# Gate sums of a two-block decoder kernel: both fp16 parts in one TensorE product of 176 columns, joined by ScalarE and VectorE

## What is computed

```python
        q = (xb @ w_query).astype(jnp.float32).reshape(t, PEER_HEADS, 2, PEER_HALF)
        scores = jnp.einsum("thpc,hpkc->thpk", q, sk)
        s1, i1 = lax.top_k(scores[:, :, 0], PEER_TOPK)
        s2, i2 = lax.top_k(scores[:, :, 1], PEER_TOPK)
        ...
        idx = jnp.take_along_axis(cand_idx, top_pos, axis=-1)
        gate = jax.nn.softmax(top_s, axis=-1)
        u = expert_down[idx]
        v = expert_up[idx]
        act = jax.nn.gelu(jnp.einsum("td,thkd->thk", xb, u).astype(jnp.float32), approximate=False)
        return jnp.einsum("thk,thkd->td", (gate * act).astype(v.dtype), v)
```

## Time and profile before

| | |
|---|---|
| Runs | 1342.95, 1343.41, 1344.96 us; median 1343.41 us |
| Profiled execution | 1341.96 us, span of its instructions 1340.2 us |
| Busy in the span | TensorE 98%, its weight loads 90%, VectorE 70%, ScalarE 54%, GpSimd 37% |
| Mean granted TensorE clock | 0.994 of full speed |

### The profile page before, as it was taken

The page is one execution under the profiler, slowest core; times in us unless marked ns, Lnnn a source line. Parts: engine busy times, 40 slices in busy tenths (PEclk is TensorE's granted clock), DMA queues, the critical chain, the costliest instruction groups (busy, mean ns, idle before and its releaser), DMA issues. The chain is left out here.

```text
span 1340.2 us, 25360 instructions
## 1 busy us (share of the span) xinstructions
PE 1314.9 (98%) x8845; PEld 1200.1 (90%) x8845; DVE 943.3 (70%) x1768; ACT 725.5 (54%) x1075; POOL 497.0 (37%) x276
## 2 busy tenths in 40 slices
PE   8899999999999999999999999999999999999997
PEld 8899799999999999998888887888889888999986
DVE  6867577999898467775666666666667667666665
ACT  6832556777777753334444444444465446444446
POOL 1010000888887888887777884000000000000000
PEclk9999999999999999999999999999999999999999
DMA  6439634666666765557777777666664324555552
GB/s 227 146 139 372 268 128 157 189 168 186 180 188 188 188 170 145 157 145 195 208 211 207 209 207 242 219 236 230 220 247 162 126 105 179 189 189 188 180 181 81
DMA packets 89805, 253.02 MB, mean 189 GB/s; under 512 B 41056, under 2 KB 57568, under 8 KB 62992
## 3 DMA queue, kind: packets, MB, share of 16 engines
q1 hardware_dynamic: 47712, 229.23, 48.6%
q0 software_dynamic: 42032, 22.99, 10.8%
HBM read 234.23 MB, written 17.96 MB: 188 GB/s over the span
## 5 line engine op out<-in xcount | busy, mean ns | idle before, releaser
L455 DVE TENSOR_TENSOR wlo<-raw,whi 128x1024 fp32r<-128x1024 f32 x412 | 502.6, 1223 | 166.1 <-ACT whi L442 154.7
L442 ACT ACTIVATE whi<-raw 128x1024 fp32r<-128x1024 f32 x412 | 434.8, 1059 | 336.2 <-PE ps L461 275.7
L408 POOL DMA_INDIRECT gates_dense<-gate,spot x256 | 485.5, 1897 | 165.7 <-issue 78.4
L459 PE MATMUL ps<-ahi,whi 128*128 128x256 f32 x1824 | 523.9, 287 | 3.9 <-DVE alo L536 3.6
L460 PE MATMUL ps<-alo,whi 128*128 128x256 f32 x1824 | 517.0, 283 | 0.0
L461 PE MATMUL ps<-ahi,wlo 128*128 128x256 f32 x1824 | 516.8, 283 | 0.0
L459 PEld LDWEIGHTS ps<-ahi,whi 128*128 128x128 f32 x1824 | 351.1, 192 | 8.8 <-issue 6.7
L460 PEld LDWEIGHTS ps<-alo,whi 128*128 128x128 f32 x1824 | 350.8, 192 | 0.9
L461 PEld LDWEIGHTS ps<-ahi,wlo 128*128 128x128 f32 x1824 | 350.5, 192 | 0.0
L459 PE MATMUL ps<-whi,phi 128*128 128x512 f32 x600 | 238.4, 397 | 2.3 <-DVE plo L1849 2.2
L461 PE MATMUL ps<-whi,plo 128*128 128x512 f32 x600 | 237.9, 396 | 0.0
(11 more groups left out here) (369 smaller groups left out, 1090.3 us busy)
## 6 DMA issues: line engine op xcount, KB each, us to landing
raw<-in_wts SPq DMA_DIRECT2D x205, 1024.0 KB, 4.8
gates_dense<-pf POOLq DMA_DIRECT2D x4, 4096.0 KB, 29.8
gd<-gates_dense SPq DMA_DIRECT2D x22, 256.0 KB
gd<-gates_dense SPq DMA_DIRECT2D x10, 512.0 KB
gates_dense<-gate,spot POOLq DMA_INDIRECT x256
cst<-in_c POOLq DMA_DIRECT2D x1, 1216.0 KB, 7.5
xt<-in_x_tok SPq DMA_DIRECT2D x2, 512.0 KB, 4.6
raw<-in_wts SPq DMA_DIRECT2D x2, 512.0 KB, 4.7
```

What stands on the lines that cost most here:

```text
L408: pl.indirect_dma_start(out=dense, out_offset=bass.IndirectOffsetOnAxis(ap=spot[:, tb, h, k:k + 1], axis=0), in_=gate[:, tb, h, k:k + 1], ...
L442: nc.scalar.activation(whi[:, j, :], raw_tile(j // 2, j % 2), ACT.Copy).then_inc(s["w_hi"], 1)
L455: nc.vector.tensor_tensor(wlo[:, j, :], raw_tile(j // 2, j % 2), whi[:, j, :].bitcast(F32), ALU.subtract).then_inc(s["w_lo"], 1)
L459: nc.tensor.matmul(out_ap, wh, xh, start=first, stop=False, skip_group_check=True)
```

## The change

A token's two matmuls become one, of 2 x 88 columns: the sum over the high parts and the sum over the low parts come out side by side and have to be added afterwards. Four tokens of 176 columns take both banks, two tokens each. ScalarE copies the high sums to SBUF, divided by 2^15 (`high_sums`). VectorE adds the low sums to them and then multiplies `ea` with the result. The low gated keys are made by ScalarE, with four small products (`low_keys_gated`), where VectorE made both parts with one. The low part of the gate is kept in fp32 as `g_low`. Both fp16 parts of a key stay as they were.

```diff
+        def group_part(q):
+            return late(2, 2 * 512).rearrange("p (b n) -> p b n", b=2)[:, :, q * 2 * SPLIT:(q + 1) * 2 * SPLIT]
+        def by_bank(j):
+            return g_sum[:, j, :, :].rearrange("p (b t) e -> p b (t e)", b=2)
...
             def gate_group(j):
                 for t in range(GT):
-                    for part in range(2):
-                        m = tm(late(2 + j, SPLIT, base=t * SPLIT), oh2[:, j, :, t], oh1[:, j, part, :, t],
-                               start=part == 0, stop=part == 1)
+                    both = late(2 + t // 2, 4 * SPLIT).rearrange("p (q t e) -> p q t e", q=2, t=2)
+                    m = tm(both[:, :, t % 2, :], oh2[:, j, :, t], oh1[:, j, :, :, t], start=True, stop=True)
...
                     pe.wait_ge(s["oh1"], i * 4 + (n + 1))
-                    if not first or n >= 2:
-                        pe.wait_ge(s["g_mul"], i * 4 + (n - 1))
+                    pe.wait_ge(s["oh1_low"], i * 4 + (n + 1))
+                    if not first or n >= 1:
+                        pe.wait_ge(s["g_both"], i * 4 + n)
                     gate_group(n % 2)
...
+            def high_sums(g, j):
+                act.wait_ge(s["g_ps"], g + 1)
+                if not isinstance(g, int) or g >= 2:
+                    act.wait_ge(s["g_mul"], g - 1)
+                A(by_bank(j), group_part(0), ACT.Copy, scale=1.0 / GATE_UP).then_inc(s["g_high"], 1)
+            def low_keys_gated(g, j):
+                act.wait_ge(s["oh_eq"], g + 1)
+                act.wait_ge(s["gate_parts"], 1)
+                for k in range(GT):
+                    t = g * GT + k
+                    v = g_low[:, t:t + 1] if isinstance(t, int) else g_low[:, bass.ds(t, 1)]
+                    m = A(oh1[:, j, 1, :, k], oheq[:, j, :, k], ACT.Copy, scale=v)
+                m.then_inc(s["oh1_low"], 1)
...
-            with act.Fori(GROUPS_AT // 4, N_EXP // 4 - 1) as i:
+            for n in range(GROUPS_AT, GROUPS_AT + 4):
+                high_sums(n - GROUPS_AT, n % 2)
+                gelu(n)
+                low_keys_gated(n + 2 - GROUPS_AT, n % 2)
+            with act.Fori(GROUPS_AT // 4 + 1, N_EXP // 4 - 2) as i:
                 for n in range(4):
+                    high_sums(i * 4 + (n - GROUPS_AT), n % 2)
                     gelu(n, i)
+                    low_keys_gated(i * 4 + (n + 2 - GROUPS_AT), n % 2)
+            for n in range(N_EXP - 8, N_EXP - 4):
+                high_sums(n - GROUPS_AT, n % 2)
+                gelu(n)
+                if n < N_EXP - 6:
+                    low_keys_gated(n + 2 - GROUPS_AT, n % 2)
...
-                V.tensor_tensor(oh1[:, j, :, :, :], oheq[:, j, :, :].unsqueeze(1).to_broadcast([P, 2, SPLIT, GT]),
-                                v.unsqueeze(2).to_broadcast([P, 2, SPLIT, GT]), ALU.mult).then_inc(s["oh1"], 1)
+                v = gT[:, 0, t:t + GT] if isinstance(t, int) else gT[:, 0, bass.ds(t, GT)]
+                V.tensor_tensor(oh1[:, j, 0, :, :], oheq[:, j, :, :], m3(v, SPLIT), ALU.mult).then_inc(s["oh1"], 1)
...
-                V.scalar_tensor_tensor(v, v, 1.0 / GATE_UP, late(2 + n % 2, GT * SPLIT).rearrange("p (t e) -> p e t", t=GT),
-                                       ALU.mult, ALU.mult)\
-                 .then_inc(s["g_mul"], 1)
+                dve.wait_ge(s["g_high"], g + 1)
+                V.scalar_tensor_tensor(by_bank(n % 2), group_part(1), 1.0 / GATE_UP, by_bank(n % 2), ALU.mult, ALU.add)\
+                 .then_inc(s["g_both"], 1)
+                dve.wait_ge(s["g_both"], g + 1)
+                V.tensor_tensor(v, v, g_sum[:, n % 2, :, :].rearrange("p t e -> p e t"), ALU.mult).then_inc(s["g_mul"], 1)
...
                 for n in range(4):
+                    apply_gates(n, i)
                     split_lo(dve, None, (base + n) % 4, i + (base + n) // 4)
                     if not last or n < 2:
                         lay_out(n + 2, i)
-                    apply_gates(n, i)
```

More of the change, by code:

```diff
@@ L93 @@
 s1_sb vn_ps vn_sb o_ps o_sq o_ss o_ms o_sqrt mix_dn pooled pool_ps mix_pool sc_ps scores cv_ready
-cv_exp zero_ok zeroed count_in pick scat0 scat1 gd0 gd1 idxT idxT_sb gate_parts oh_eq oh1 g_ps g_mul gelu p_hi p_split s_ps s_max s_exp
+cv_exp zero_ok zeroed count_in pick scat0 scat1 gd0 gd1 idxT idxT_sb gate_parts oh_eq oh1 oh1_low g_high g_both g_ps g_mul gelu p_hi p_split s_ps s_max s_exp
 s_norm pt_ps pt_sb ao_ps ao_sb v_sb rs_ps rs_sb ro_ps rxc r_sq r_ms r_sqrt mix_ret evac2 rg_done ff_conv
@@ L158, in program @@
         oh1 = place("oh1", [2, 2, SPLIT, GT], F16, at=aux)
+        g_low = place("g_low", [P], at=aux)
+        g_sum = place("g_sum", [2, GT, SPLIT], at=aux)
         assert aux[0] <= small + 4 * KT * T
@@ L1296, in _ @@
                         gelu(n, i, True)
+            def high_sums(g, j):
[11 more added lines that the diff above has]
+                m.then_inc(s["oh1_low"], 1)
             for n in range(CHOSEN_AT, GROUPS_AT):
                 gelu(n)
+                if n >= GROUPS_AT - 2:
+                    low_keys_gated(n - (GROUPS_AT - 2), n % 2)
                 if n == CHOSEN_AT:
@@ L1790, in first_keys_gated @@
                 dve.wait_ge(s["oh_eq"], g + 1)
-                v = gT[:, :, t:t + GT] if isinstance(t, int) else gT[:, :, bass.ds(t, GT)]
-                V.tensor_tensor(oh1[:, j, :, :, :], oheq[:, j, :, :].unsqueeze(1).to_broadcast([P, 2, SPLIT, GT]),
-                                v.unsqueeze(2).to_broadcast([P, 2, SPLIT, GT]), ALU.mult).then_inc(s["oh1"], 1)
+                v = gT[:, 0, t:t + GT] if isinstance(t, int) else gT[:, 0, bass.ds(t, GT)]
+                V.tensor_tensor(oh1[:, j, 0, :, :], oheq[:, j, :, :], m3(v, SPLIT), ALU.mult).then_inc(s["oh1"], 1)
             def lay_out(n, i=None):
@@ L1807, in apply_gates @@
                 v = ea[:, 0:SPLIT, P + t:P + t + GT] if isinstance(t, int) else ea[:, 0:SPLIT, bass.ds(t + P, GT)]
-                V.scalar_tensor_tensor(v, v, 1.0 / GATE_UP, late(2 + n % 2, GT * SPLIT).rearrange("p (t e) -> p e t", t=GT),
-                                       ALU.mult, ALU.mult)\
-                 .then_inc(s["g_mul"], 1)
+                dve.wait_ge(s["g_high"], g + 1)
[3 more added lines that the diff above has]
+                V.tensor_tensor(v, v, g_sum[:, n % 2, :, :].rearrange("p t e -> p e t"), ALU.mult).then_inc(s["g_mul"], 1)
             dve.wait_ge(s["idxT_sb"], 1)
-            V.scalar_tensor_tensor(gT[:, 1, :], late(2, P, base=2 * P), GATE_UP, gT[:, 0, :], ALU.mult, ALU.subtract)
+            V.scalar_tensor_tensor(g_low[:, :], late(2, P, base=2 * P), GATE_UP, gT[:, 0, :], ALU.mult, ALU.subtract)
             V.tensor_copy(iota[:, :, :], b3(count[:, 0:P], GT)).then_inc(s["gate_parts"], 1)
```

## The result

The changed kernel takes 1384.49 us (median of 4 runs, 1382.15 to 1384.69) against 1343.31 us for the kernel before on the same chip (4 runs, 1342.95 to 1344.96): ratio 1.0309, interval 1.0296 to 1.0321. It is slower, as forecast, but by 41 us in place of 26.7; the range ended at 1382. The profiled execution took 1384.6 us, its span is 1382.8.

What follows compares the result with a forecast made beforehand. It took TensorE to bound the kernel before, and a ring of waits the changed one: 4.50 us a round over 30 rounds put group 31 26.7 us later, 1343.4 + 26.7 = 1370 us, range 1361 to 1382.

Steps and rivals of the forecast that it cites:

- the sign: Whole kernel: slower, given 0.96, against 0.01 for the same and 0.03 for faster.
- the ring: Gate stage: ScalarE's and VectorE's queued waits close a loop once per step, 4.50 us from high sums to high sums.
- high sums to joining: Ring term: ScalarE's high sums 0.46 us, then 0.04 us to VectorE.
- joining to product: Ring term on VectorE: sum of the parts 0.514 us, then a wait with register work of 0.12 us.
- product to tile split: Ring term on VectorE: product with ea 0.52 us, of which 0.08 overlaps what follows, so 0.44 us.
- low keys to high sums: Ring term on ScalarE: four overlapping low products of 0.25 us each, 1.0 us.
- product with ea out of SBUF ... 0.52 us for 352: VectorE's product behind the sum, priced between L1845's 256- and 128-column rows at 1.05 ns a column: 0.52 us.
- I take 176/256 of 0.12 ... 0.35 us. That saves 0.26 us a step: TensorE's gate matmuls: four of 176 columns take 0.35 us where eight took 0.61, saving 0.26 us a step.
- rival of a faster kernel at 1335 us: Gate stage: ring not felt, TensorE sets a step of 3.31 us, 8.3 us less, 1335 us; 3 in 100.
- Low products at full length: ScalarE's low keys: products do not overlap, 5.0 us a round or more, 1385 us; 6 in 100.
- The bank rotation: Rule that independent groups go round through different PSUM banks; the change gives it up, by itself no price forecast.
- rival of a falling clock: TensorE's granted clock falls in the gate stage as TensorE idles; with half the steps, about 1401 us; 4 in 100.

Runs made afterwards that it cites:

- e6: Changed kernel with ScalarE making the low keys of group n+1 ahead of the hidden-tile wait, not those of n+2 behind gelu: 1343.23 us, ratio 1.001.
- e5: Changed kernel with each token's sums 256 columns apart in PSUM, read there with a stride, and g_sum written and read side by side: 1376.19 us, ratio 1.0245.
- e7: Changed kernel with the edits of e5 and e6 together: 1342.57 us, ratio 0.9997 to the kernel before.
- e12: e7 with eight gate products of 88 columns in place of four of 176: 1341.11 us, ratio 0.9995 to the kernel before.
- e9: e7 with the gated keys (moving operand) stored side by side per token, not 8 bytes apart: 1337.43 us, ratio 0.9966 to the kernel before.
- e3: Changed kernel with VectorE's old order, applying the gates behind the tile split and one-hots: 1399.05 us, ratio 1.0423 to the kernel before.
- e8: Changed kernel with VectorE's old order as in e3 and the early low keys of e6: 1392.02 us, ratio 1.0368 to the kernel before.
- e13: Kernel before with only the gated keys stored side by side per token, not 8 bytes apart: 1334.43 us, ratio 0.9938.
- e10: e7 with the one-hot weights of a token stored side by side, not 8 bytes apart: 1341.53 us, ratio 0.9996 to the kernel before.
- e15: e9 with VectorE's key product in its old element order, reading side by side and writing 352 bytes apart: 1371.43 us, ratio 1.0221 to the kernel before.
- e1: Changed kernel with g_sum stored in the order the product with ea reads, its writers going 16 bytes apart: 1395.58 us, ratio 1.0394.
- e14: Changed kernel with only the gated keys stored side by side per token: 1382.83 us, ratio 1.0303 to the kernel before.
- e11: Changed kernel with VectorE's old order as in e3 and ScalarE's high sums moved behind the tile's high part: 1376.04 us, ratio 1.0247.

## Why the prediction was wrong

**The mechanism and the sign were right.** TensorE waits for g_sum ahead of each group, VectorE for g_sum 1.36 us (1.3 forecast), ScalarE for `oheq` ahead of the low keys and, but for the last group, never for TensorE ahead of the high sums. e6 moves one link and the loss is gone.

**What failed is the size of the ring, 4.50 us for 5.00.** By its terms, forecast and then measured, in us: high sums to joining 0.50, 0.61; joining to product 0.634, 0.66; product to tile split 0.44, 0.71; split 1.14, 1.14; to the key one-hots 0.34, 0.34; to the low keys 0.45, 0.46; low keys to high sums 1.00, 1.08. The differences add up to 0.50. 30 rounds of it would be 15.0 us. Group 31 came at 640.84 for 627.3, 13.5 later: the first high sums came 0.8 us before the forecast 491.21, and the first four rounds and the last two were 4.79 to 4.92 us. The median missed by 14.5.

**The largest of these, 0.27 us, is the step "product with ea out of SBUF ... 0.52 us for 352" from the earlier trace rows.** Those rows of L1845 read both operands side by side; g_sum is read 352 bytes apart. L1808 had a step of 352 bytes too, but out of PSUM, where e5 shows that even 1 KB is free, and so hid the difference. The Trainium skill has this price, which I didn't weigh: page "Vector Engine (DVE) Microarchitecture Reference", section Measured stream behaviour on trn2, gives 1.054 ns an element with all operands side by side, and 1.73 with one source that hops 4 KiB at every element. By that page, as an estimate, 352 elements take 0.24 us more, and the traces agree (789 less 527 ns, 0.26), though the hop here is 352 bytes.

The other terms are small: the wait for the high sums and their length directly behind the low keys (503 ns, against 465 behind a wait in e7) gave 0.11; low keys 0.27 us apart for 0.25 gave 0.08.

**A second step failed without being seen in the total: TensorE's "I take 176/256 of 0.12 ... 0.35 us. That saves 0.26 us a step".** Four products take 0.51 us, and of the 0.10 us that are left the products around them take more than half (e12 against e7). Under the ring this hardly showed, since the prediction's sum held it once and not per step, but the rival of a faster kernel at 1335 us rested on it: e7 has no ring and stands at 1342.57. The 0.35 was scaled from fp32 products whose moving operand (`ahi`) lies side by side; the gate's keys do not. With them side by side the four start 0.077 us apart (e9), close to the forecast 0.08.

**The rivals.** "Low products at full length", 5.0 us and 1385 us, gave the measured time, and it is still not the cause: they start 0.27 us apart, not 0.375. The clock didn't fall in the changed kernel (1.00 in the stage). The bank rotation of the Trainium skill, page "Perfetto Trace Analysis", was given no price by itself. With VectorE's new order that held (e6); in the old order the wait that the shared banks bring is a link of a ring of 5.22 us (e3, e8), so that this price holds for one order alone.

The 2.2 us more behind group 31 were not looked into; the kernels of the experiments differ by as much there.

## What to carry to other kernels

Write down, for every wait that a change adds, what stands behind it in that engine's queue, follow this until it closes, and price each link; then try to move the one link that has another place to stand, since one block of ScalarE moved by a few instructions was worth 41 us here and half as many gate products 0.04 us a step. When a duration is borrowed from a row, compare more than the shape: the memory (PSUM or SBUF) and the step between elements of each operand, on the writing side above all. And before products are merged, see whether it is their number or the layout of the moving operand that sets their pace: the layout alone took the kernel before from 1342.2 to 1334.4 us.

## What the runs showed of the hardware

- TensorE, fp16 moving operand 8 bytes apart against side by side: 334 and 240 ns for 176 columns, 0.152 and 0.077 us apart; 261 and 209 ns for 88 columns (e12, e13). The Trainium skill, page "Advanced Engine Details and Errata", section Memory Cachelines, asks for at least two hits on a 16-byte line for full performance. 8 bytes apart are two to a line, and here that was not full: a difference between page and trace in which the trace decides. Weights 8 bytes apart cost the products nothing (e10: 332 ns).
- VectorE, SBUF: one source 352 bytes apart in fp32 0.26 us more for 352 elements; fp16 read 8 bytes apart 0.18 more for 352 (e9), 0.26 for 512 (e10) and 0.36 for 704 (e13, 0.89 for 0.53), that is 1.04 ns for each further element in place of 0.52 (the operand it is combined with is read in another order too, and the two weren't told apart); fp16 written 352 bytes apart 1.44 us more for 352 (e15). ScalarE's fp32 write 16 bytes apart cost 0.33 us more for 352 (e1, 836 ns for 503). PSUM read out of order cost nothing on either (e5).
- The granted clock. Between 495 and 600 us TensorE waited 1.58 us ahead of each gate group in e14, and 1.56 in e8 in the steps at full clock; still the first kept its full 2.4 GHz and the second spent a part of the stretch at 1.2 GHz. The two rows, e14 first (columns of the earlier trace rows):
```profile
495.00:600.00 105.00, 71.59 (x596) 67.88 (x597) 76.43 (x128) 58.30 (x149) 88.38 (x51) 1.00 0.47 109
```
```profile
495.00:600.00 105.00, 83.92 (x564) 78.08 (x563) 67.59 (x120) 59.59 (x141) 91.40 (x41) 0.89 0.42 101
```
Which difference between them decides wasn't tried. e3 stood at 0.87, e1 at 0.89 and e11 at 0.90; the forecast's rival of a falling clock was thus nearer than its 4 in 100 had it.
